# Streaming mixer and mixture-of-experts layer, float32, one core: sixteen 1 MB weight places, a TensorE loop written out for four experts, and lookup tables made ahead of it

## What is computed

```python
def _moe(h, router_w, router_b, exp_w_gate, exp_b_gate, exp_w_up, exp_b_up, exp_w_down, exp_b_down):
    t = h.reshape(B * L, D_MODEL)
    logits = (t @ router_w + router_b).astype(jnp.float32)
    top_vals, top_idx = lax.top_k(logits, TOP_K)          # 4 of 32 experts
    top_w = jax.nn.softmax(top_vals, axis=-1)
    ...
    for e in range(N_EXPERTS):                            # 32
        gt = jnp.minimum(t @ exp_w_gate[e] + exp_b_gate[e], SWIGLU_LIMIT)
        up = jnp.clip(t @ exp_w_up[e] + exp_b_up[e], -SWIGLU_LIMIT, SWIGLU_LIMIT)
        act = gt * jax.nn.sigmoid(SWIGLU_ALPHA * gt) * (up + 1.0)
        out = out + combine[:, e:e + 1] * (act @ exp_w_down[e] + exp_b_down[e]).astype(jnp.float32)
```

## Time and profile before

| | us |
|---|---|
| median of 3 runs | 1213.97 (1212.2 to 1214.23) |
| the profiled execution, its own time | 1206.91 |
| its span, first to last instruction | 1205.2 |
| TensorE busy in the span | 1166.7 (97%) |
| VectorE, ScalarE, GpSimd busy | 405.7, 182.4, 74.3 |
| weight pairs of the experts | 192 loads of 2048 KB |
| DMA traffic over the span | 456.05 MB, mean 378 GB/s |

### The profile page before, as it was taken

The page is one execution under the profiler, slowest core; times in us unless marked ns, Lnnn a source line. Parts: engine busy times, 40 slices in busy tenths (PEclk is TensorE's granted clock), DMA queues, the critical chain, the costliest instruction groups (busy, mean ns, idle before and its releaser), DMA issues.

```text
span 1205.2 us, 16544 instructions
## 1 busy us (share of the span) xinstructions
PE 1166.7 (97%) x6133; PEld 478.7 (40%) x6133; DVE 405.7 (34%) x894; ACT 182.4 (15%) x305; POOL 74.3 (6%) x83
## 2 busy tenths in 40 slices
PE   8999999999999999999999999999999999999993
PEld 5676665533333333333333333333333333333331
DVE  3497225632222322232222222222223222222227
ACT  2101301211111111111111111111111111111112
POOL 4069200200000000000000000000000000000000
PEclk9999999999999999999999999999999999999997
DMA  9968664589999999999999699999999999999992
GB/s 345 373 240 305 235 245 157 201 324 417 430 427 429 429 429 428 429 429 429 428 429 402 258 404 431 427 428 427 431 428 428 427 430 428 429 427 430 429 429 88
DMA packets 53662, 456.05 MB, mean 378 GB/s; under 512 B 5321, under 2 KB 20229, under 8 KB 27019
## 3 DMA queue, kind: packets, MB, share of 16 engines
q1 hardware_dynamic: 51392, 452.87, 90.9%
q10 hardware_dynamic: 2251, 2.93, 0.8%
HBM read 454.38 MB, written 1.40 MB: 378 GB/s over the span
## 4 chain that ended last, share of the span: by engine, by line
PE 75%; DMA 19%; DVE 2%; ACT 1%; SPq 1%; issue 1%; DVEq 0%; POOLq 0%
PE bank L1590 45%; DMA ring<-in_exp_w_gate 18%; PE bank L1358 5%; PE bank L1624 5%; PE bank L1307 4%; PE bank L1541 4%; PE bank L1461 2%; PE bank L1580 2%; PE bank L1549 1%; PE bank L1445 1%; DMA ring<-in_w_ada 1%; PE bank L1277 1%; ACT arena L739 1%; PE bank L1611 1%; SPq L416 1%; PE bank L1555 1%
## 5 line engine op out<-in xcount | busy, mean ns | idle before, releaser
L1590 PE MATMUL bank<-ring,arena 128*64 128x512 f32 x3168 | 704.2, 596 | 9.5 <-POOLq L555 8.4
L1590 PEld LDWEIGHTS bank<-ring,arena 128*64 128x64 f32 x3168 | 221.9, 137 | 447.9 <-issue 406.2
L1120 DVE TENSOR_SCALAR arena<-bank 128x512 f32<-128x512 f32 x33 | 22.8, 692 | 355.3 <-PE bank L1590 355.3
L1105 DVE TENSOR_TENSOR arena<-arena,bank 128x512 f32<-128x512 f32 x132 | 84.8, 684 | 108.2 <-PE bank L1624 77.6
L739 ACT ACTIVATE arena<-bank 128x512 f32<-128x512 f32 x33 | 19.7, 597 | 375.2 <-PE bank L1555 375.2
L1624 PE MATMUL bank<-arena 64*128 64x512 f32 x264 | 74.5, 641 | 0.2 <-DVE arena L1101 0.2
L1541 PE MATMUL bank<-h,arena 128*64 128x512 f32 x272 | 64.4, 593 | 0.2 <-DVE arena L994 0.2
L1358 PE MATMUL bank<-arena,ring 128*128 128x288 f32 x256 | 63.9, 408 | 0.0
L868 DVE SCALAR_TENSOR_TENSOR h<-h,dwc 128x318 f32<-128x318 f32 x120 | 55.6, 574 | 0.0
L1358 PEld LDWEIGHTS bank<-arena,ring 128*128 128x128 f32 x256 | 48.2, 190 | 14.7 <-issue 1.7
L737 ACT ACTIVATE arena<-arena 128x512 f32<-128x512 f32 x33 | 20.8, 630 | 198.7 <-DVE arena L1120 198.7
(11 more groups left out here) (304 smaller groups left out, 737.1 us busy)
## 6 DMA issues: line engine op xcount, KB each, us to landing
ring<-in_exp_w_down SPq DMA_DIRECT2D x64, 2048.0 KB, 18.1
ring<-in_exp_w_gate SPq DMA_DIRECT2D x64, 2048.0 KB, 19.7
ring<-in_exp_w_up SPq DMA_DIRECT2D x64, 2048.0 KB, 20.4
ring<-in_w_ada SPq DMA_DIRECT2D x24, 1024.0 KB, 10.1
ring<-in_gate_w SPq DMA_DIRECT2D x8, 1024.0 KB, 7.5
ring<-in_w_in SPq DMA_DIRECT2D x6, 1024.0 KB, 19.0
ring<-in_w_out SPq DMA_DIRECT2D x4, 1024.0 KB, 6.3
ring<-in_conv_w_out SPq DMA_DIRECT2D x2, 1024.0 KB, 7.9
```

What stands on the lines that cost most here:

```text
L1105: ins = v.tensor_tensor(acc[:, t, cs], acc[:, t, cs], bank[6 + hh][:, :], ALU.add)
L1590: ins = mm(out[64 * hh:64 * hh + 64, :], lhs(k), ring[:, s, D * (k % 2) + HALF * hh:D * (k % 2) + HALF * (hh + 1)], start=(done is y_mm an ...
```

## The change

- Two more pairs of places, 16 in all. They lie in `arena`, which grows from 15088 to 17660 floats per partition and takes in small buffers that had places of their own: `EARLY_PAIR` at its end, `LATE_PAIR` from 7168, where the output projection's buffers lie. Pair q of the running count goes to place q % 8.
- SyncE issues the first pair of expert 1 ahead of expert 0's fourth pair, after three waits, and its second pair after the last router product (`logit_mm`); it loads on in a loop of 24 pairs (four experts), in which each pair waits for the pair that stood 8 before it.
- GpSimd's loop and `weights_ready` go. TensorE waits for the pair's own semaphore, once a pair.
- TensorE's loop runs over 8 groups of four experts; the four are written out, each with an inner loop over its items and two register loads from `base_i` ahead of it. Item 0 is in the loop.
- The tables are made ahead of the items: the count sums ahead of `turn_tokens(0)`, the owner sums behind it. The transposed routing tables (`routedT`, `ohwT`), which TensorE and ScalarE made in item 0, are made by VectorE with a transpose and ten copies. `acc` is zeroed by ScalarE instead of GpSimd.
- `g2b` and `fgb` are loaded when all items of expert 30 are done, to ring places 0 and 1.

```diff
+ARENA = 17660
+EARLY_PAIR, LATE_PAIR = ARENA - 4096, 7168
 RING = 12
+PAIRS = 8
+PER_EXPERT = 6
...
-COUNT_BANK, OWNER_BANK = 5, 1
+ROUTED_COPIES = 8
+COUNT_BANK, OWNER_BANK = 5, 2
...
-        arena = sb("arena", [P, 15088])
+        arena = sb("arena", [P, ARENA])
...
-        acc = view(2304, TT, D)
+        acc = view(2304, 2, D)
...
-        actT = view(6912, HALF)
+        actT = view(4608, HALF)
...
-        fgb = view(12664, D)
+        fgb = ring[:, 1, 0:D]
...
+        def slots(q, k):
+
+            if q < RING:
+                return ring[:, q:q + k, :].rearrange("p s n -> p (s n)")
+            at = (EARLY_PAIR, LATE_PAIR)[(q - RING) // 2] + SLOT * (q % 2)
+            return arena[:, at:at + SLOT * k]
...
+        far_ld = [sem(f"far_ld{i}") for i in range(2)]
+        pair_ld = slot_ld[0:RING:2] + far_ld
...
+            def load(e, q):
+
+                i, p = q % PER_EXPERT, q % PAIRS
+                w = (wg_v, wu_v, wd_v)[i // 2]
+                sp.dma_start(slots(2 * p, 2), w[e][:, i % 2, :]).then_inc(pair_ld[p], 16)
...
-            for i in sorted(range(0, PIECES, 2), key=front_use):
-                expert(0, lambda _: front_use(i), (i,))
+            order = sorted(range(PER_EXPERT), key=front_use)
+            for i in order:
+                if i == order[3]:
+
+                    sp.wait_ge(act_c_ready, 1)
+                    sp.wait_ge(cst_mm, 4)
+                    sp.wait_ge(rows_out[1], 64)
+                    load(1, PER_EXPERT)
+                sp.wait_ge(piece_used, front_use(i))
+                load(0, i)
+            sp.wait_ge(logit_mm, TT)
+            load(1, PER_EXPERT + 1)
             sp.wait_ge(base_ready, 1)
...
+            def refill(g, qs):
+
+                at = None
+                for q in qs:
+                    before, i = (q - PAIRS) // PER_EXPERT, (q - PAIRS) % PER_EXPERT
+                    if i == 0 or at is None:
+                        at = sp.value_load(base_i[0:1, bass.ds(g * 4 + (before + 1), 1)], min_val=1, max_val=MAX_ITEMS)
+                    sp.wait_ge(piece_used, at * PIECES + (F_END - PIECES + 2 * i + 2))
+                    load(g * 4 + q // PER_EXPERT, q)
+
+            with sp.Fori(0, E // 4 - 1) as g:
+                refill(g, range(PAIRS, PAIRS + 4 * PER_EXPERT))
+            refill(E // 4 - 1, range(PAIRS, 4 * PER_EXPERT))
+            at = sp.value_load(base_i[0:1, E - 1:E], min_val=E - 1, max_val=MAX_ITEMS)
+            sp.wait_ge(piece_used, at * PIECES + (F_END - PIECES + PIECES))
...
-            with pool.Fori(1, items) as n_i:
-                e = pool.value_load(owner_i[0:1, bass.ds(n_i, 1)], min_val=0, max_val=E - 1)
-                for i in range(0, PIECES, 2):
-                    pool.wait_ge(slot_ld[i], (e + (USES[i] + 1)) * 16)
-                    pool.sem_inc(weights_ready, 2)
...
-            act.wait_ge(ohwT_mm, 1)
-            a.activation(ohwT, bank[2][:, 0:TT * P], ACT.Copy).then_inc(ohwT_ev, 1)
-            for i in range(2):
-                act.wait_ge(routedT_mm, i + 1)
-                a.activation(routedT[:, i, :], bank[7 - i][LOOKUP, 0:TOK], ACT.Copy).then_inc(routedT_ready, 1)
+            act.wait_ge(h2_ready, TT)
+            act.wait_ge(h2_last, 1)
+            a.activation(acc_all, ones[:, 0:1].broadcast_to([P, 2 * D + D // 4]), ACT.Copy, scale=0.0).then_inc(acc_zero, 1)
...
+            dve.wait_ge(ssq2, 6)
+            v.memset(ohwT, 0.0).then_inc(ohwT_zero, 1)
+            step(v.transpose(turned.rearrange("p (a t) j -> p a t j", a=2), routed[:, :, :, 0:E]))
+            for q in range(4):
+                m = TT if q == 0 else 2
+                for i in range(2):
+                    at = TOK * i + 32 * q
+                    dst = biases[LOOKUP, 0, at:at + P * m].rearrange("p (t n) -> p t n", t=m)[:, :, 0:32]
+                    v.tensor_copy(dst, turned[32 * q:32 * q + 32, TT * i:TT * i + m, :]).then_inc(routedT_ready, 1)
+            dve.wait_ge(routedT_ready, ROUTED_COPIES)
+            dve.wait_ge(ohwT_zero, 1)
+            v.tensor_copy(ohwT[0:E, 0:TOK], routedT[:, 1, :])
+            v.tensor_copy(ohwT[SLOTS:SLOTS + E, 0:TOK], routedT[:, 1, :]).then_inc(ohwT_ev, 1)
+            items = dve.value_load(base_i[0:1, E:E + 1], min_val=E, max_val=MAX_ITEMS)
...
-            def product(out, lhs, n_i, c0, done, mid=None, before_used=None):
+            def product(out, lhs, g, j, c0, done, mid=None, before_used=None):
 
                 for k in range(KD):
                     s = c0 + k // 2
-                    if k % 2 == 0:
-                        pe.wait_ge(weights_ready, n_i * PIECES + (s + 1))
+                    if k % 4 == 0:
+                        q = PER_EXPERT * j + s // 2
+                        used = USES[2 * (q % PAIRS)] if 2 * (q % PAIRS) < RING else 0
+                        pe.wait_ge(pair_ld[q % PAIRS], g * 48 + 16 * (used + q // PAIRS + 1))
+                    w = slots((PIECES * j + s) % (2 * PAIRS), 1)
...
+            pe.wait_ge(count_ready, 1)
+            mm(bank[COUNT_BANK][:, E:2 * E], count_b, upto[0:E, 0:E], start=True, stop=True)
+            mm(bank[COUNT_BANK][0:E, 2 * E:2 * E + 4], upto[0:E, 0:E], count_b[:, 0:4], start=True, stop=True).then_inc(table_mm, 1)
             turn_tokens(0)
 
-            def tables_1():
...
+            pe.wait_ge(begun_ready, 1)
+            owners = bank[OWNER_BANK]
...
-            item(0, tables_1, tables_2)
+
             pe.wait_ge(base_ready, 1)
+            with pe.Fori(0, E // 4) as g:
+                for j in range(4):
+                    first_item = pe.value_load(base_i[0:1, bass.ds(g * 4 + j, 1)], min_val=0, max_val=MAX_ITEMS)
+                    next_first = pe.value_load(base_i[0:1, bass.ds(g * 4 + (j + 1), 1)], min_val=1, max_val=MAX_ITEMS)
+                    with pe.Fori(first_item, next_first) as n:
+                        item(n, g, j)
             items = pe.value_load(base_i[0:1, E:E + 1], min_val=E, max_val=MAX_ITEMS)
-            with pe.Fori(1, items) as n:
-                item(n)
```

More of the change, by code:

```diff
@@ L178, in build @@
         ohwT = view(6400, TT * P)
-        acc_s = acc[:, 2, 0:D // 4]
+        acc_s = view(2304 + 2 * D, D // 4)
+        acc_all = view(2304, 2 * D + D // 4)
         acc_row = view(0, D)[0:NS_TOK, :]
@@ L416, in _ @@
                 sp.dma_start(dst, src).then_inc(slot_ld[f % RING], 16)
-            def expert(e, last_use, pieces=range(0, PIECES, 2)):
-                for i in pieces:
-                    sp.wait_ge(piece_used, last_use(i + 1))
-                    w = (wg_v, wu_v, wd_v)[i // 4]
-                    sp.dma_start(ring[:, i:i + 2, :].rearrange("p s n -> p (s n)"), w[e][:, i % 4 // 2, :]).then_inc(slot_ld[i], 16)
-            def front_use(i):
-                return max(f for f in range(N_FRONT) if f % RING in (i, i + 1)) + 1
@@ L428, in _ @@
-            for i in sorted(range(0, PIECES, 2), key=front_use):
-                expert(0, lambda _: front_use(i), (i,))
-            sp.wait_ge(base_ready, 1)
-            with sp.Fori(1, E) as e:
-                at = sp.value_load(base_i[0:1, bass.ds(e, 1)], min_val=1, max_val=MAX_ITEMS)
-                expert(e, lambda i: at * PIECES + (F_END - PIECES + i + 1))
-            at = sp.value_load(base_i[0:1, E:E + 1], min_val=E, max_val=MAX_ITEMS)
-            sp.wait_ge(piece_used, at * PIECES + (F_END - PIECES + 1))
@@ L530, in _ @@
             pool.wait_ge(pm_mm, KD)
[L531 to L532 removed]
+            g.memset(ysb, 0.0).then_inc(ysb_zero, 1)
             pool.wait_ge(spread_ld[1], 64)
@@ L540, in _ @@
             g.tensor_tensor(h2[:, 1, cs], h2[:, 1, cs], sh2b[:, 0, cs], ALU.add).then_inc(h2_last, 1)
-            pool.wait_ge(h2_last, 1)
-            pool.wait_ge(h2_ready, TT)
-            g.memset(acc, 0.0).then_inc(acc_zero, 1)
-            for i in range(0, PIECES, 2):
-                pool.wait_ge(slot_ld[i], (USES[i] + 1) * 16)
-                pool.sem_inc(weights_ready, 2)
-            pool.wait_ge(base_ready, 1)
-            items = pool.value_load(base_i[0:1, E:E + 1], min_val=E, max_val=MAX_ITEMS)
-            pool.wait_ge(owner_ready, 1)
-            with pool.Fori(1, items) as n_i:
-                e = pool.value_load(owner_i[0:1, bass.ds(n_i, 1)], min_val=0, max_val=E - 1)
-                for i in range(0, PIECES, 2):
-                    pool.wait_ge(slot_ld[i], (e + (USES[i] + 1)) * 16)
-                    pool.sem_inc(weights_ready, 2)
         @block.scalar
@@ L960, in add_output @@
                     dve.wait_ge(x2_ready, after)
-                parts = [view(13812 + cs.start, cs.stop - cs.start)[0:r, :] for cs, _ in cuts]
+                parts = [view(12288 + cs.start, cs.stop - cs.start)[0:r, :] for cs, _ in cuts]
                 for part, (cs, src) in zip(parts, cuts):
@@ L1084, in _ @@
                             ALU.is_ge).then_inc(begun_ready, 1)
-            dve.wait_ge(base_ready, 1)
-            items = dve.value_load(base_i[0:1, E:E + 1], min_val=E, max_val=MAX_ITEMS)
```

(21 more changed lines are left out.)

117 lines of the change are left out of this document (48 added, 69 removed).

## The result

The changed kernel takes **1197.24 us** (median of 4 runs, 1195.22 to 1198.37), the kernel before beside it 1213.09 us (4 runs, 1211.85 to 1214.23). The ratio is 0.9871, with an interval of 0.9853 to 0.9889: 15.9 us, or 1.3%, faster. The prediction of 1199.5 us was right in sign and lies 2.3 us above the result. The profiled execution of the changed kernel took 1198.37 us with a span of 1196.6 us.

What follows compares the result with a forecast made beforehand. The prediction took weight loads, 29.37 us per expert against 28.21 us of TensorE work, as the bound once their lead is used up; 10.6 + 1.6 + 0 + 2.3 = 14.5 us off 1213.97 gave 1199.5 us, range 1192 to 1210.

Steps and rivals of the forecast that it cites:

- The sum: Whole kernel: gains of 10.6, 1.6, 0 and 2.3 us, together 14.5 us, taken from a median of 1213.97 us.
- Part 1: Weight loads in the items: sixteen places let loads run further ahead, TensorE never waits for weights; gain 10.6 us.
- The offset of 7.06 us: Median of runs above the profiled execution of before, taken as the same 7.06 us for both kernels.
- Part 2: Item 0 and its tables: item 0 starts 2.2 us later and is 3.8 us shorter; gain 1.6 us.
- the sign of slow tables: Item 0: a length over 22 us would show that VectorE's tables hold it up.
- Part 3: TensorE's loop form: 1.5 us of register work per expert stays hidden; gain or loss 0 us.
- The lead of 4.3 us: Item's end: TensorE's sequencer is 4.3 us ahead of the matrix engine, hiding the loop's 1.5 us of register work.
- the 15 packets: TensorE's instruction queue: some 15 packets if code stays at hand, 40 or more if it is fetched.
- The two rivals on code: Loop's eight branches back: fetch partly hidden, 0 to 13.6 us lost, chance 0.17; fetch queued behind weights, chance 0.07.
- the slower rival: Loop's branches back: code fetch queued behind weights, at 9 us each a loss of 50 us, 1249 us; chance 0.07.
- Part 4: Kernel's end: `g2b` issued a whole item earlier, so VectorE no longer waits 2.64 us for it; gain 2.3 us.
- no wait for `g2b`: Kernel's end: VectorE never waits for `g2b`, named as a sign that the forecast is right.

Runs made afterwards that it cites:

- `b_turn`: The kernel before, with GpSimd's pooling held back until VectorE's convolution is done: 1208.42 us, ratio 0.9991 to the kernel before.
- `a_turn`: The changed kernel, with GpSimd's pooling held back until VectorE's convolution is done: 1193.04 us, ratio 0.9863 to the kernel before.
- `b_same2`: The kernel before, unchanged, run and profiled again in another set: 1213.23 us, ratio 1.0003 to the kernel before.
- `a_lead6`: The changed kernel with all sixteen places, but each pair loaded only when the pair 6 before it has been used: 1208.47 us, ratio 0.9995 to before.
- `a_lead7`: The changed kernel with all sixteen places, but each pair loaded only when the pair 7 before it has been used: 1201.15 us, ratio 0.9907 to before.
- `a_loads`: The changed kernel with eight more register loads, values unused, ahead of each expert's inner loop: 1311.5 us (one run).
- `a_eight`: The changed kernel with TensorE's loop written out for eight experts instead of four: 1213.95 us (one run).
- `a_same`: The changed kernel, unchanged, run and profiled again: 1197.66 us, ratio 0.9869 to the kernel before.
- `a_late`: `a_warm` with `g2b` and the final norm's weights issued later, when the last item has begun: 1192.69 us, ratio 0.9834 to the kernel before.
- `a_warm`: `a_turn` with five short unused identity products in TensorE's pauses before item 0: 1192.03 us, ratio 0.9827 to the kernel before.

## Why the prediction was right, point by point

**The sum.** Forecast 14.5 us, measured 15.9 between the medians, 15.4 between `b_turn` and `a_turn`, 14.9 between the profiles of `b_same2` and the changed kernel. Part 1 is its bulk and was right; parts 2 and 4 came near for reasons other than those given, which was luck. The other 0.9 us of the miss are the median of before, 1213.97 then and 1213.09 now.

**The offset of 7.06 us** between the median and the profiled time of before was assumed to be the same for both kernels. For the changed kernel it is 1197.24 - 1198.37 = -1.1 us. The profile of before had caught the first picture of the convolution (and a full clock in the stretch of 20 to 30 us, 1.00, where `b_same2` and the changed kernel have 0.83). The forecast came out all the same because both medians carry the second picture; but its own steps would have put the profiled time at 1192.4 us, and it is 1198.37. The prediction saw the 7 us and looked only to the weights for them.

**Part 1, the lead: right.** 10.6 us forecast, 11.6 measured (11.5 between `b_turn` and `a_turn`). 10.6 is for items of 28.21 us; they take (1170.74 - 268.93) / 32 = 28.18. The mean of the first ten is 28.17, and why is open. No wait for weights is left, and `a_lead6` takes the whole term away, `a_lead7` a quarter.

**Part 2, item 0: right in sign, 1.6 forecast, 0.9 measured, 2.6 between `b_turn` and `a_turn`; two errors against each other.** Item 0's start was to be 2.2 us later and is 1.0 later (5.31 instead of 4.31 us behind the rank sum). The step that failed is `count_b`. It was read as 4.1 us behind the rank sum, and it is 1.7. In the trace of before, an operation on 32 x 5 elements stood 2.60 us beside GpSimd's zeroing of `acc`:

```profile
234.84 2.70 POOL L543 MEMSET arena<- 128x3072 f32 x1 [0.96 <-DVE h L1052]
...
234.96 2.60 DVE L1059 TENSOR_SCALAR rt<-fills,bank 32x5 f32<-32x5 f32 x1
```

The change takes that memset from GpSimd, and the prediction had written that nobody waited for GpSimd there. VectorE now, in the changed kernel:

```profile
241.63 0.21 DVE L1072 TENSOR_SCALAR rt<-fills,bank 32x5 f32<-32x5 f32 x1
...
242.06 0.27 DVE L1074 TENSOR_SCALAR arena<-ones,rt 32x128 f32<-32x128 f32 x1
...
250.15 0.30 DVE L1111 COPY arena<-biases 32x288 f32<-32x288 f32 x1
251.74 0.23 DVE L1136 TENSOR_SCALAR item_col<-routed,first 128x3 f32 x1 [1.29 <-issue]
```

From `count_b` to the gate product, on the other hand, 3.6 us pass instead of 2.45. Item 0's length was to fall by 3.8 us to 21.1. It is 21.27 in `a_turn`, as forecast, but 22.97 in the profile of the changed kernel, where its gate product took 8.78 us instead of 7.09: TensorE's clock was 0.64 and 0.50 in the four microseconds from 246 on. So 22.97 us is over the 22 us which the prediction named as the sign of slow tables, but the tables were not the cause. The clock drop, which no term of the prediction had, takes 1.7 us of the 2.6. VectorE's added tables cost nothing, as forecast: it is in its loop at 251.7 us, later than the 248 named, and the gate product ends at 254.7.

**Part 3, the loop's form: right.** 0 us. The lead of 4.3 us is shown by `a_loads` to 0.2 us, the 15 packets are there, and no branch was slow. The two rivals on code were the right thing to fear: had the code not stayed, eight branches at the 6.2 us of `a_eight` would have cost about 49 us (an estimate), and the change would have ended at some 1247 us, where the slower rival had it.

**Part 4, the end: 2.3 us forecast, 2.7 measured, 1.7 between `b_turn` and `a_turn`, for another reason.** `g2b` is not issued a whole item earlier. It is issued 1170.74 - 1150.49 = 20.2 us ahead of the last down product, and it was 20.1 before. What changed is how long it takes to land, 21.5 us where it was 24.3, since the weights ahead of it are no longer late. The end of TensorE's and VectorE's work (start, us, what):

```profile
1172.25 1.16 DVE L1165 COPY arena<-arena 32x256 f32<-32x256 f32 x4
...
1178.71 1.99 PE L1724 MATMUL bank<-arena 64*128 64x512 f32 x8 [0.88 <-ACT arena L758]
...
1180.37 1.29 DVE L1187 TENSOR_TENSOR arena<-bank,ring 128x512 f32<-128x512 f32 x2
```

VectorE is free about when the scatter's first results are there, as forecast. But "no wait for `g2b`" holds just barely, in this profile alone: it lands at 1172.04 us, VectorE starts on it at 1172.25. `a_same` waits for it again, where the kernel before waits 2.64 us:

```profile
DVE arena L1165 <- DMA ring<-mod_rows: 0.8, 1, 0.8
```

`a_turn` waits 0.6 us, and that is why its end gains less. `a_late` shows that the issue time is worth nothing. So this term hangs on part 1; with `a_lead6` it vanished too (28.35 us).

**A better version.** `a_turn` and `a_warm` beat both kernels. The one edit that is shown to do it is to hold GpSimd's pooling back: `a_turn` takes 1193.04 us and the unedited change 1197.66, in another set; against the kernel before it is 0.9827 in `a_warm` and 0.9869 in `a_same`. That is some 5 us.

## What to carry to other kernels

Where loads and work have nearly the same period, count the late items between two pauses of the loads and multiply by the difference: that tells how many places are enough, to within a couple of microseconds. Before writing a loop out, multiply its code by the copies and keep the product below what is known to stay at hand, and compare the loop's register work with the sequencer's lead at the branch. Look at one profiled execution's own time beside the median before summing up: where they differ by more than the runs scatter, the profile shows another picture than the runs have, and a second profile of the same kernel is the cheapest experiment.

## What the runs showed of the hardware that was not expected

- A jump back over some 77 KB of TensorE's code costs nothing (0.23 us at most, 15 instruction packets), one over some 154 KB costs 6.1 to 6.8 us at the branch with the DMA engines full, and 6.2 us of TensorE's time after the lead of 4.3 us, 1.9 of it by the clock (one run each).
- VectorE and GpSimd beside each other have two stable outcomes with the same program: 38.9 us for one addition of GpSimd and 27.7 us for 60 steps of VectorE, or additions that get through and 34.1 us for the steps. By the times, which one comes stays the same over most runs of a set and changes between sets; what decides it is open.
- A memset of 2.7 us on GpSimd held a VectorE operation on 32 x 5 elements for 2.60 us; without it, it takes 0.21 us.
- A gap of 2.3 us or of 3.9 to 4.6 us was followed by products at the lower clock (the statistics products 4.61 instead of 2.41 us, 32 gate products 8.78 to 9.51 instead of 7.09), but of the 31 gaps of 2.64 to 3.27 us in `a_loads` only nine were, and a longer gap was not more often among them than a short one. In item 0 the same drop came in two profiles (8.78 and 8.48 us) and stayed away in others with the same idle time of 0.89 us before it.
- Items of the changed kernel take 28.14 to 28.22 us, in turns, where those of before took 28.21. No run here says why.
